# Products of the gated attention's output projection moved between the heads of the last state-space tile, sums of squares one part later, and a projection that waits tile by tile

## The chip, the core and the metric

One core of one Trainium2 chip runs the whole program in one launch. The metric is the device time of one execution in microseconds (us). A core has five engines with queues of their own: PE (TensorE, matmuls), ACT (ScalarE), DVE (VectorE), POOL (GpSimd) and SP (SyncE, which issues DMAs); semaphores order them. TensorE's clock is granted by a throttle, at 2.4 GHz (shown as 1.00) or 1.2 GHz (0.50).

## What is computed

One decoder layer on 592 tokens (16 meta, 512 of a prompt, 8 sequences of 8 sample tokens), in float32. Two mixers run side by side and their outputs are projected together:

```python
o_gla = rmsnorm(o, gla_norm_w) * silu(g)                 # gated linear attention, 512 wide
y = rmsnorm(y_ssd * silu(z), ssd_norm_w)                 # state-space mixer, 512 wide
mix = concatenate([o_gla, y])
h = h + mix @ w_out                                      # 1024 x 1024
h = h + peer(rmsnorm(h, norm2_w), ...)                   # 16384 experts, 16 picks for each of 8 heads
```

The last line is the long part of the program (from about 480 us on); the change lies ahead of it, where `mix @ w_out` is made.

## The kernel before

Tokens lie along the columns: `h`, `xn` and `mix` are 128 x 8 x 592, worked on in two halves of 296 columns. For the mixers the tokens are cut into five tiles, four of 128 and the last, the sample tile, of 80 (16 prompt tokens and the 8 sequences).

The output projection is split over its input. `mix[:, 0:4]` is the attention's half and is ready first; `project_gla(k)` makes part k (of 8 parts of 128 output features) from it: 2 halves x 4 blocks, eight full products of 128x128 by 128x296, into banks 6 and 7. The profile shows each product as two passes, so one part is x16. ScalarE copies part k out of the banks (`copy_gla_out(k)`, semaphore `half_copied`), and part k + 1 may only start then, since it writes the same banks. GpSimd adds the copied parts to the residual `h`, which is loaded again into its place once the state-space output is copied (`y_copied`, then `x_reloaded`). `mix[:, 4:8]` is the state-space half. It is ready after the last tile and a norm: VectorE multiplies by silu(z), ScalarE squares, PE sums the squares with a matmul by ones (`norm_sum`, bank 4 and 5), ScalarE takes the square roots, VectorE the reciprocals and then the normalised values (`norm(1)`, semaphore `normed`). Then `project_ssd(k)` makes part k from it, eight full products again, and VectorE adds them to `h`.

The order on each engine is written out by hand. On PE, before: for tile i the decay matrices of the next tile, `project_gla(i)`, then the eight heads of tile i, two matmuls each. The sample tile's heads are longer: one matmul by `L` (80 columns), one by `H` (16 columns) and eight by `Hsm` (8 columns each, the states of the eight sequences), all with 64 output rows. After the loop:

```python
project_gla(TILES)                       # part 5
pe.wait_ge(y_copied, TILES)
for k in range(4):
    norm_sum(1, k)
project_gla(TILES + 1)                   # part 6
project_gla(TILES + 2)                   # part 7
pe.wait_ge(half_copied, KT)
pe.wait_ge(normed, norm_base[1] + 4)
```

and then `project_ssd(0)` to `project_ssd(7)`, with the state updates of the eight sequences (`to_state`) and the sums of squares of the next norm between them. ScalarE's order is: copies of parts 0 to 5, the four squares and two square roots of `norm(1)`, copies of parts 6 and 7.

Lines of the kernel before: L807 product of `project_gla`, L834 and L836 or L841 the heads, L855 product of `project_ssd`, L795 `to_state`, L565 `norm_sum`, L579 the input projections between the attention's chunks, L1163 `copy_gla_out`, L1059 squares, L1062 square roots, L1354 reciprocals, L1364 normalised values, L1606 the multiplication by silu(z), L1864 GpSimd's additions, L1025 the product of the experts' second stage.

## Time and profile before

| | us |
|---|---|
| median of 3 runs | 2017.6 |
| lowest and highest | 2016.31 and 2018.34 |
| the profiled execution | 2015.8 |
| its span, first to last instruction | 2014.0 |
| PE busy in it | 1979.7 |
| VectorE, ScalarE, GpSimd busy | 1211.4, 636.2, 1105.9 |

The span is the profiled execution's own; what is counted against it is counted against 2015.8. PE is busy nearly all the time, so an engine's busy share tells little here; the views that tell more are the chain of waits (what released each piece of work), the timeline (start, duration, engine, line, and in brackets the idle time before it and what ended it) and the windows (busy time of each engine and the granted clock of PE in a stretch). Where a timeline row has x16, it merges sixteen instructions; its end is modelled for matmuls, so the start of the next row is the better end.

### The profile page before, as it was taken

The page shows a single profiled execution, that of the slowest core. Times are in us where ns is not written, and L with a number is a line of the kernel's source. Part 1 is how long each engine was busy: PE and PEld are TensorE (multiplying, and loading weights), DVE is VectorE, ACT ScalarE, POOL GpSimd, SP SyncE. Part 2 cuts the span into 40 slices and gives each one's busy share as a digit, 9 for nine tenths or more (in the row PEclk, how much of TensorE's full clock was granted, in tenths as well). Part 3 has the DMA queues.
Part 4 walks back from the last instruction along what each step waited for, and adds up shares of the span by engine and source line. Part 5 has one row for each costly group of instructions (what it writes and reads, how often), then busy time and mean ns, then how long its engine had stood idle before and what let it go on. Part 6 is the DMA issues. An engine that isn't in the chain of part 4 may idle for free.

```text
span 2014.0 us, 28921 instructions
## 1 busy us (share of the span) xinstructions
PE 1979.7 (98%) x11021; PEld 1772.3 (88%) x11021; DVE 1211.4 (60%) x2243; ACT 636.2 (32%) x935; POOL 1105.9 (55%) x694
## 2 busy tenths in 40 slices
PE   8999999999999999999999999999999999999997
PEld 4678778868999999999999999998999999999996
DVE  4425365646897787778343441114677777777775
ACT  3324123323333232332323333223333333333332
POOL 0113220222358786888888888865566666666310
PEclk8999999999999999999999999999999999999999
DMA  3396003032335455555555555778999999999971
GB/s 152 107 339 203 32 32 89 1 111 101 102 122 122 131 113 141 120 131 131 130 130 120 127 123 125 173 191 284 320 330 325 328 326 327 324 329 323 332 257 49
DMA packets 237285, 365.17 MB, mean 181 GB/s; under 512 B 87777, under 2 KB 178418, under 8 KB 236530
## 3 DMA queue, kind: packets, MB, share of 16 engines
q1 hardware_dynamic: 163570, 294.37, 43.9%
q0 software_dynamic: 72448, 67.41, 16.2%
q10 hardware_dynamic: 1152, 1.84, 0.3%
q8 instruction: 74, 1.21, 0.2%
q14 instruction: 41, 0.34, 0.0%
HBM read 290.15 MB, written 73.38 MB: 181 GB/s over the span
## 4 chain that ended last, share of the span: by engine, by line
PE 95%; DVE 2%; ACT 1%; DMA 1%; SPq 0%; issue 0%; ACTq 0%; POOL 0%; DVEq 0%; POOLq 0%
PE bank L1025 31%; PE bank L941 30%; PE bank L579 9%; PE bank L950 9%; PE bank L885 2%; PE bank L599 2%; PE bank L855 2%; PE bank L807 1%; PE bank L701 1%; PE bank L565 1%; PE bank L672 1%; PE bank L717 1%; PE bank L932 1%; PE bank L985 1%; PE bank L841 1%; DMA ring<-in_v 1%
## 5 line engine op out<-in xcount | busy, mean ns | idle before, releaser
L1886 POOL DMA_INDIRECT gates_scratch<-gate_val,gate_at x384 | 642.7, 1674 | 139.3 <-issue 115.5
L1025 PE MATMUL bank<-W,vsp 128*128 128x448 f32 x3072 | 624.6, 366 | 2.8 <-DVE W L1767 2.8
L1025 PEld LDWEIGHTS bank<-W,vsp 128*128 128x128 f32 x3072 | 578.1, 188 | 48.8 <-issue 3.0
L941 PE MATMUL bank<-xh,usp 128*128 128x448 f32 x2048 | 593.9, 366 | 0.0
L941 PEld LDWEIGHTS bank<-xh,usp 128*128 128x128 f32 x2048 | 384.7, 188 | 30.7 <-ACT gl L1239 0.4
L941 PE MATMUL bank<-xl,usp 128*128 128x448 f32 x1024 | 374.0, 365 | 0.0
L1652 DVE TENSOR_TENSOR usp<-ring,usp 128x1024 fp32r<-128x1024 f32 x120 | 144.5, 1221 | 329.2 <-ACT usp L1217 329.0
L1762 DVE TENSOR_TENSOR vsp<-ring,vsp 128x1024 fp32r<-128x1024 f32 x128 | 157.0, 1227 | 178.6 <-ACT vsp L1304 178.6
L1905 POOL DMA_INDIRECT picked<-in_v,row_index x128 | 149.5, 1168 | 185.5 <-DVE acc L1781 163.0
L1912 POOL DMA_INDIRECT hid_b<-own_hidden_scratch,hid_index x128 | 189.6, 1481 | 63.7 <-issue 38.7
L941 PEld LDWEIGHTS bank<-xl,usp 128*128 128x128 f32 x1024 | 192.5, 188 | 14.2
L579 PE MATMUL bank<-xn,ring 128*128 128x296 f32 x640 | 202.5, 439 | 0.0
L1239 ACT ACTIVATE gl<-bank 128x448 f32<-128x448 f32 x128 | 69.8, 545 | 398.2 <-PE bank L941 398.1
L950 PE MATMUL bank<-usp,xh 128*128 128x256 f32 x1024 | 194.6, 283 | 0.0
L1304 ACT ACTIVATE vsp<-ring 128x1024 fp32r<-128x1024 f32 x128 | 135.7, 1060 | 185.8 <-PE bank L1025 171.1
L950 PEld LDWEIGHTS bank<-usp,xh 128*128 128x128 f32 x1024 | 163.0, 190 | 0.8
L1781 DVE SCALAR_TENSOR_TENSOR acc<-picked,w_b,acc 128x1024 f32<-128x1024 f32 x126 | 160.6, 1280 | 0.2
L1308 ACT ACTIVATE W<-sq 128x448 fp32r<-128x448 f32 x128 | 74.2, 580 | 233.9 <-DVE sq L1757 230.4
L950 PE MATMUL bank<-usp,xl 128*128 128x256 f32 x512 | 144.8, 283 | 0.0
L1217 ACT ACTIVATE usp<-ring 128x1024 fp32r<-128x1024 f32 x128 | 128.2, 1051 | 0.3 <-DMA ring<-in_u 0.3
L579 PEld LDWEIGHTS bank<-xn,ring 128*128 128x128 f32 x640 | 107.8, 191 | 23.2 <-issue 7.3
L1833 POOL TENSOR_TENSOR E<-E,qT 128x2048 f32<-128x2048 f32 (+1 forms) x7 | 29.1, 4159 | 158.0 <-ACT qT L1068 91.2
(278 smaller groups left out, 2054.3 us busy)
## 6 DMA issues: line engine op xcount, KB each, us to landing
ring<-in_u SPq DMA_DIRECT2D x128, 512.0 KB, 3.7
ring<-in_v SPq DMA_DIRECT2D x128, 512.0 KB, 5.6
hidden_scratch<-gl SPq DMA_DIRECT2D x128, 224.0 KB, 1.9
xn<-hidden_scratch SPq DMA_DIRECT2D x128, 224.0 KB, 5.8
G<-gates_scratch SPq DMA_DIRECT2D x120, 224.0 KB, 4.8
gates_scratch<-zero SPq DMA_DIRECT2D x32, 768.0 KB, 8.7
ring<-in_wproj SPq DMA_DIRECT2D x36, 512.0 KB, 4.3
own_hidden_scratch<-glo SPq DMA_DIRECT2D x64, 128.0 KB, 1.7
```

The source lines that it names most:

```text
L579: mm = pe.matmul(bank[2 * (n % 2) + x][:, 0:half], ring[:, n % 4, k * P:(k + 1) * P], src[:, k, at + x * half:at + (x + 1) * half], start= ...
L941: mm = pe.matmul(bank[b][:, 0:TA], w, src[:, k, 0:TA], start=(k == 0 and w is hi and src is xh), stop=(k == KT - 1 and w is lo))
L950: mm = pe.matmul(bank[b][:, 0:2 * P].rearrange("t (a e) -> t a e", a=2), src[:, k, TA:TP], u, start=(k == 0 and u is hi and src is xh), st ...
L1025: mm = pe.matmul(bank[(k + 4) % 8][:, 0:TA], w, W[:, n % 4, z, :], start=(n == 0 and w is hi and z == 0), stop=(n == NE - 1 and w is lo))
L1217: act.activation(usp[:, u_slot(j), 0, :], ring[:, j, :], ACT.Copy).then_inc(uhi_ready, 1)
L1304: act.activation(vsp[:, n % 4, 0, :], ring[:, n % 4, :], ACT.Copy).then_inc(vhi_ready, 1)
L1652: dve.tensor_tensor(usp[:, u_slot(n), 1, :], ring[:, n % 4, :], usp[:, u_slot(n), 0, :].bitcast(F32), ALU.subtract).then_inc(ulo_ready, 1)
L1762: dve.tensor_tensor(vsp[:, n % 4, 1, :], ring[:, n % 4, :], vsp[:, n % 4, 0, :].bitcast(F32), ALU.subtract).then_inc(vlo_ready, 1)
L1781: ins = dve.scalar_tensor_tensor(acc[:, x % 2, :], picked[:, x % NROW, :], w_b[:, x:x + 1], acc[:, x % 2, :], ALU.mult, ALU.add)
L1886: pool.indirect_dma_start(gates_flat, bass.IndirectOffsetOnAxis(ap=gate_at[0:r, i, x:x + 1], axis=0), gate_val[0:r, i, hh, x - hh * TOPK:x ...
L1905: pool.indirect_dma_start(picked[:, x % NROW, :], None, rows_of_v, bass.IndirectOffsetOnAxis(ap=row_index[:, x:x + 1], axis=0)).then_inc(r ...
L1912: pool.indirect_dma_start(hid_b[:, x:x + 1], None, own_flat, bass.IndirectOffsetOnAxis(ap=hid_index[:, x:x + 1], axis=0)).then_inc(picked_ ...
```

## The change

Three edits, in two of the engine programs. (1) `project_gla` can make a part in pieces, and part 5 is made in six pieces between the sample tile's heads: one product after each of heads 1 to 4, two after each of heads 5 and 6. (2) Behind the tile PE makes part 6 and then the sums of squares, where part 5 stood ahead of them; ScalarE copies part 6 between the squares and the square roots of `norm(1)`. (3) `project_ssd(0)` no longer waits for all four normalised tiles, but before each of its first four products for the tile that this product reads.

```diff
-            def project_gla(k):
+            def project_gla(k, first=0, count=2 * GH):
 
-                pe.wait_ge(ring_loaded[k // 2], 16 * (N_FEAT // 4 + 1))
-                if k >= 1:
-                    pe.wait_ge(half_copied, k)
-                for x in range(2):
-                    for c in range(GH):
-                        a = k % 2 * (D // 2) + c * P
-                        mm = pe.matmul(bank[6 + x][:, 0:HALF], ring[:, k // 2, a:a + P], mix[:, c, x * HALF:(x + 1) * HALF],
-                                       start=(c == 0), stop=(c == GH - 1))
-                mm.then_inc(part_done, 1)
+                if first == 0:
+                    pe.wait_ge(ring_loaded[k // 2], 16 * (N_FEAT // 4 + 1))
+                    if k >= 1:
+                        pe.wait_ge(half_copied, k)
+                for m in range(first, first + count):
+                    x, c = m // GH, m % GH
+                    a = k % 2 * (D // 2) + c * P
+                    mm = pe.matmul(bank[6 + x][:, 0:HALF], ring[:, k // 2, a:a + P], mix[:, c, x * HALF:(x + 1) * HALF],
+                                   start=(c == 0), stop=(c == GH - 1))
+                if first + count == 2 * GH:
+                    mm.then_inc(part_done, 1)
...
+                        if 1 <= hh < SH - 1:
+                            project_gla(TILES, first=hh - 1 if hh < 5 else 2 * hh - 6, count=1 if hh < 5 else 2)
...
                 for x in range(2):
                     for c in range(4):
+                        if k == 0 and x == 0:
+                            pe.wait_ge(normed, norm_base[1] + c + 1)
                         a = k % 2 * (D // 2) + c * P
...
-            project_gla(TILES)
+            project_gla(TILES + 1)
             pe.wait_ge(y_copied, TILES)
             for k in range(4):
                 norm_sum(1, k)
-            project_gla(TILES + 1)
             project_gla(TILES + 2)
             pe.wait_ge(half_copied, KT)
-            pe.wait_ge(normed, norm_base[1] + 4)
...
                     act.activation(sq[:, k % 2, :], src[:, off + k, :], ACT.Square).then_inc(sq_ready, 1)
+                if m == 1:
+                    copy_gla_out(TILES + 1)
                 act.wait_ge(sq_used, norm_base[m] + n)
...
             norm(1, lambda k: act.wait_ge(yz_ready, k + 1))
-            copy_gla_out(TILES + 1)
             copy_gla_out(TILES + 2)
```

The lines behind the edits move by two to six: L807 becomes L808, L834 and L841 become L836 and L843, L855 becomes L861, and on ScalarE L1059, L1062 and L1163 become L1063, L1068 and L1169.

On PE, the first three heads of the sample tile, in the kernel before (each row is a line, the operation, its output and inputs, their shape, and the semaphores that it waits for):

```order
L834 MATMUL bank<-L,Xd 64x80 [waits y_copied,h_updated,xw_ready,hsm_keys_loaded,ct_ready,m_ready]
L841 MATMUL bank<-Ct,H 64x16
L841 MATMUL bank<-Ct,Hsm 64x8 x8
L834 MATMUL bank<-L,Xd 64x80
L841 MATMUL bank<-Ct,H 64x16
L841 MATMUL bank<-Ct,Hsm 64x8 x8
L834 MATMUL bank<-L,Xd 64x80
L841 MATMUL bank<-Ct,H 64x16
L841 MATMUL bank<-Ct,Hsm 64x8 x8
```

and in the changed kernel:

```order
L836 MATMUL bank<-L,Xd 64x80 [waits y_copied,h_updated,xw_ready,hsm_keys_loaded,ct_ready,m_ready]
L843 MATMUL bank<-Ct,H 64x16
L843 MATMUL bank<-Ct,Hsm 64x8 x8
L836 MATMUL bank<-L,Xd 64x80
L843 MATMUL bank<-Ct,H 64x16
L843 MATMUL bank<-Ct,Hsm 64x8 x8
L808 MATMUL bank<-mix,ring 128x296 [waits half_copied,ring_loaded2]
L836 MATMUL bank<-L,Xd 64x80
L843 MATMUL bank<-Ct,H 64x16
L843 MATMUL bank<-Ct,Hsm 64x8 x8
L808 MATMUL bank<-mix,ring 128x296
```

Heads 0 and 1 still stand together; from then on a product of `project_gla(5)` stands behind each head, and the first of them carries the waits that stood at the part's start.

On PE, from the last head to the first product of the state-space projection, before:

```order
L841 MATMUL bank<-Ct,Hsm 64x8 x8
L807 MATMUL bank<-mix,ring 128x296 [waits half_copied,ring_loaded2]
L807 MATMUL bank<-mix,ring 128x296 x7
L565 MATMUL bank<-sq,ones_sb 128x296 [waits sq_ready,y_copied]
L565 MATMUL bank<-sq,ones_sb 128x296
...
L565 MATMUL bank<-sq,ones_sb 128x296 [waits sq_ready]
L565 MATMUL bank<-sq,ones_sb 128x296
L807 MATMUL bank<-mix,ring 128x296 [waits half_copied,ring_loaded3]
L807 MATMUL bank<-mix,ring 128x296 x7
L807 MATMUL bank<-mix,ring 128x296 [waits half_copied,ring_loaded3]
L807 MATMUL bank<-mix,ring 128x296 x7
L855 MATMUL bank<-mix,ring 128x296 [waits ring_loaded0,proj_act,normed,half_copied]
L855 MATMUL bank<-mix,ring 128x296 x7
```

and in the changed kernel:

```order
L843 MATMUL bank<-Ct,Hsm 64x8 x8
L808 MATMUL bank<-mix,ring 128x296 [waits half_copied,ring_loaded3]
L808 MATMUL bank<-mix,ring 128x296 x7
L565 MATMUL bank<-sq,ones_sb 128x296 [waits sq_ready,y_copied]
L565 MATMUL bank<-sq,ones_sb 128x296
...
L565 MATMUL bank<-sq,ones_sb 128x296 [waits sq_ready]
L565 MATMUL bank<-sq,ones_sb 128x296
L808 MATMUL bank<-mix,ring 128x296 [waits half_copied,ring_loaded3]
L808 MATMUL bank<-mix,ring 128x296 x7
L861 MATMUL bank<-mix,ring 128x296 [waits proj_act,normed,ring_loaded0,half_copied]
L861 MATMUL bank<-mix,ring 128x296 [waits normed] x3
L861 MATMUL bank<-mix,ring 128x296 x4
```

Part 6 (the one with ring_loaded3) now comes ahead of the sums of squares, and the single wait for all tiles at L855 has become four waits.

On ScalarE, from the squares of `norm(1)` to the copy of part 7, before:

```order
L1059 ACTIVATE sq<-mix 128x592 [waits yz_ready] x2
L1059 ACTIVATE sq<-mix 128x592 [waits sq_used,yz_ready] x2
L1062 ACT_TABLE_LOAD
L1062 ACTIVATE sq<-bank,eps_sb 128x296 [waits sq_used]
L1062 ACTIVATE sq<-bank,eps_sb 128x296
L1163 ACTIVATE sg<-bank 128x296 [waits part_done]
L1163 ACTIVATE sg<-bank 128x296
L1163 ACTIVATE sg<-bank 128x296 [waits part_done]
L1163 ACTIVATE sg<-bank 128x296
```

and in the changed kernel:

```order
L1063 ACTIVATE sq<-mix 128x592 [waits yz_ready] x2
L1063 ACTIVATE sq<-mix 128x592 [waits sq_used,yz_ready] x2
L1169 ACTIVATE sg<-bank 128x296 [waits part_done]
L1169 ACTIVATE sg<-bank 128x296
L1068 ACT_TABLE_LOAD
L1068 ACTIVATE sq<-bank,eps_sb 128x296 [waits sq_used]
L1068 ACTIVATE sq<-bank,eps_sb 128x296
L1169 ACTIVATE sg<-bank 128x296 [waits part_done]
L1169 ACTIVATE sg<-bank 128x296
```

The copy of part 6 stands ahead of the table load and the square roots.

## Rows read from the trace of the kernel before

**Rows 1.** The page's first part, busy time by engine.
```profile
PE 1979.7 (98%) x11021; PEld 1772.3 (88%) x11021; DVE 1211.4 (60%) x2243; ACT 636.2 (32%) x935; POOL 1105.9 (55%) x694
```

**Rows 2.** The chain of waits, 390 to 480 us: start us, us, what.
```profile
402.59 6.47 PE bank L807 x16
409.08 0.73 ACT E L1163 x2
...
410.53 4.34 PE bank L565 x16
...
419.77 4.24 PE bank L807 x16
...
424.89 4.22 PE bank L855 x16
```

**Rows 3.** Windows, from:to, length, PE busy (count), granted clock, DMA share, GB/s.
```profile
311.00:325.00 14.00, 14.00 (x107) 1.00 0.00 0
...
393.00:394.00 1.00, 1.00 (x19) 0.74 0.00 0
398.00:400.00 2.00, 2.00 (x24) 0.50 0.00 0
...
407.00:408.00 1.00, 1.00 (x5) 0.93 1.05 329
...
1366.00:1370.00 4.00, 1.15 (x9) 0.96 0.97 308
1370.00:1373.00 3.00, 3.00 (x9) 0.50 0.67 248
1373.00:1374.00 1.00, 1.00 (x6) 0.94 0.04 13
```

**Rows 4.** Timeline, the heads of the sample tile and part 5 behind them.
```profile
390.31 0.35 PE L834 MATMUL bank<-L,Xd 80*64 80x80 f32 x2
...
391.48 0.24 PE L841 MATMUL bank<-Ct,H 128*64 128x16 f32 x2
...
393.45 0.30 PE L841 MATMUL bank<-Ct,H 128*64 128x16 f32 x2
...
400.55 0.34 PE L841 MATMUL bank<-Ct,H 128*64 128x16 f32 x2
...
404.65 0.34 PEld L807 LDWEIGHTS bank<-mix,ring 128*128 128x128 f32 x1 [0.16 <-issue]
```

**Rows 5.** Timeline of PE, one chunk of the attention's sample tile.
```profile
312.54 1.26 PE L579 MATMUL bank<-xn,ring 128*128 128x296 f32 x4
...
314.67 0.52 PE L579 MATMUL bank<-xn,ring 128*128 128x296 f32 x1
```

**Rows 6.** Timeline of all engines, from the sample tile to the state-space projection.
```profile
403.58 2.83 DVE L1606 TENSOR_TENSOR mix<-mix,sz 128x592 f32<-128x592 f32 x4
...
413.58 1.28 ACT L1062 ACT_TABLE_LOAD   x1
...
414.71 4.15 PE L807 MATMUL bank<-mix,ring 128*128 128x296 f32 x16
...
415.52 4.04 DVE L1354 RECIPROCAL sq<-sq 128x296 f32<-128x296 f32 x2 [8.32 <-ACT sq L1062]
...
428.95 1.89 PE L795 MATMUL bank<-XWm,btok 80*128 80x256 f32 x8
```

**Rows 7.** Timeline in narrow windows, 412 to 425: additions (POOL) and normalisations (DVE).
```profile
412.32 8.41 POOL L1864 TENSOR_TENSOR h<-h,E 128x592 f32<-128x592 f32 x6 [29.03 <-DMA h<-in_xT]
...
419.60 1.77 DVE L1364 SCALAR_TENSOR_TENSOR mix<-mix,prm,sq 128x592 f32<-128x592 f32 x1
...
420.68 1.98 POOL L1864 TENSOR_TENSOR h<-h,sg 128x592 f32<-128x592 f32 x1
...
421.30 2.00 DVE L1364 SCALAR_TENSOR_TENSOR mix<-mix,prm,sq 128x592 f32<-128x592 f32 x1
...
423.97 0.82 DVE L1364 SCALAR_TENSOR_TENSOR mix<-mix,prm,sq 128x592 f32<-128x592 f32 x1
```

## The prediction

> **What bounds the kernel now.** I read the page first: TensorE is busy for 1979.7 of 2014.0 us [rows 1], so only idle or slow time of TensorE can be won. The chain of waits shows where it lies around the change: from the end of the sample tile at 402.5 us to the first state-space product at 424.9 it runs mostly over PE, with three holes where PE waited for ScalarE: from 409.1 to 410.5, and 0.9 us each before 419.77 and before 424.89 [rows 2]. Then I read the granted clock in windows: it falls in the window of 393 and is back at about 407.1 [rows 3]. PE was busy throughout, and what it had done before the fall was heads of the sample tile alone, ten small matmuls each. Two heads take 1.97 us at 2.4 GHz (391.48 to 393.45), 0.98 each; four take 7.10 at 1.2 GHz (to 400.55), 1.78 each. A full product of 128x296 takes 0.51 us at 2.4 GHz (eight between 424.89 and 428.95) [rows 2, 6]. At 1.2 GHz it takes 0.99: two passes of 0.34 + 0.16 us by its weight loads [rows 4]. Five slow heads lose 0.8 us each and the projection behind them 2.4 (6.47 against 4.06): 6.4 us lie there.
>
> **Edit 1, the eight products of part 5 between the heads.** No instruction is added; eight products move from behind the tile into it, one after each of heads 1 to 4, two after heads 5 and 6. Part 5's first product waits for the copy of part 4, which ScalarE makes while heads 0 and 1 run (0.73 us against 1.97): it costs nothing. ScalarE's copy of part 5 now lies beside head 7 (0.73 and a little for the signal, against 0.98): nothing either, with under 0.2 us to spare. If the clock holds, the tile ends at 390.3 + 8 x 0.98 + 8 x 0.51 = 402.2 with part 5 done, against 409.1 before [rows 2, 4]: 6.9 us ahead.
>
> Does it hold? Before shows both ends. Heads alone, with PE never idle: it fell. The chunks of the gated attention, where two full products (four passes of L579) return every 2.13 us with small matmuls between: 1.00 over 14 us [rows 3, 5]. The new pattern has one product in 1.49 us (0.34 of the time, where the attention has 0.48 and heads alone nothing), from head 5 on two in 2.0 (0.51), but two heads with none at the start. I take full speed, since most of the pattern is nearer to the attention than to heads alone.
>
> **Edit 2, sums of squares one part later.** They now stand behind part 6: 402.2 + 4.1 = 406.3. The first hole goes, since the squares need VectorE's four multiplications, of 0.75 us each from 1.1 us behind the tile on, and these run under part 6. The sums take 4.2 us as before (410.53 to 414.71) and end at 410.5; part 7 follows at once, to 414.6. PE has done by then what it had done by 423.9: 9.3 us ahead [rows 2, 6].
>
> But the next step, the normalised state-space half, hangs on three other engines. Before, the table load for the square roots began 3.05 us after the sums did and lay under the last ones. Now the copy of part 6 stands ahead of it: 406.3 + 3.05 + 0.73 = 410.1, and 1.28 for the load make 411.4, 0.9 behind the sums. The reciprocals begin 0.66 after the load's end and normalisation 4.1 later: 416.1, against 419.6 [rows 6, 7]. The Trainium skill (ScalarE: Activation LUTs, What ACT_TABLE_LOAD costs) puts a change of tables at 2.66 us, a drain included. The trace does not show that drain, since the reciprocals stood 0.66 us behind the load; with it the gain would be 1.4 us smaller.
>
> GpSimd decides the rest. It adds eight parts to the reloaded input from 412.3 on, six in 8.41 us, 1.40 each. Their start hangs on the reload, issued when the tile's output is copied, and stays at 412.1. One normalisation alone takes 0.82 us; the two that met additions took 1.77 and 2.00, and the addition between them 1.98 [rows 7]. The two engines take turns, one pair in about 1.93 us (from the end of the sixth addition, 420.73, to that of the seventh, 422.66). Two of the four met additions before; now only three are done at 416.3 and all four take turns with the rest: they end at 417.0, 418.9, 420.9 and 422.8. Against 424.8 that is 2.0 us, where the start had been 3.5 ahead.
>
> **Edit 3, the projection waits per tile.** Its first four products follow one normalisation each; the fourth and the last four come behind 422.8. At full speed that is 5 x 0.51: 425.4, against 428.95 before, a gain of 3.5 us.
>
> At full speed. But from 414.6 to 422.8 PE has three products, 1.5 us of work in 8.2, with gaps of 2.4, 1.4, 1.5 and 1.4. The nearest rows: a hole of 2.85 us (PE busy 1.15 of 4.00) behind which the clock was at 0.50 [rows 3], and single holes of 1.5 and 0.9 between dense projections, behind which eight products took 4.2 us, as at 2.4 GHz [rows 2]. Three lone products in such a stretch are nearer to the 2.85. So I take a fall near 420. In the rows the clock came back 3.3 us (1369.8 to 1373.1) and 4.6 us (402.5 to 407.1) after dense products had begun. Five products at 0.99 end at 427.8, with the clock back after 3.3 us at 427.0; I take 427.35, a gain of 1.6 us. Behind it PE goes on with the same work, almost without a hole, so the gain is carried to the end. **Sum:** the profiled execution took 2015.8 us (span 2014.0); less 1.6 that is 2014.2. The median of the runs is 1.8 above it: 2017.6 - 1.6 = 2016.0. If the clock never fell the gain is 3.5; if everything ran slow to the end of that projection, 1.1.
>
> **Rivals.**
> A. *The clock holds in the paced projection too.* For it: no single gap is as long as 2.85 us. Against it: four of 1.4 or more in a row. The gain is 3.5 us: 2014.1. The Trainium skill (TensorE: Matmul & The Clock Gate, the table under Why this matters for your kernels) ties a fall to one idle gap between bursts of matmuls; by it this case would come. The fall at 393.5 had no gap before it, which speaks against that reading.
> B. *Slower: the clock still falls between the heads*, where it fell before, in head 2. Then seven products stand in slow time too: 5.3 heads at 1.78 and 7 products at 0.99 from 393.5 on end at 409.9, 7.7 behind 402.2; part 6 loses up to 2.3 more. The reload is issued later too, so nothing is made up: 7.7 + 2.3 - 1.6 = 8.4 us slower, 2026.0. It is decided at the two heads that still stand together; if the clock fell only near head 5, about half. For it: the first 2.5 us behind 390.3 hold one product. Against it: the attention [rows 3, 5].
> C. *GpSimd and VectorE do not take turns.* Then four normalisations take 3.0 us, end at 419.1, PE has no long gap, and the projection ends at 421.7: 7.2 us, 2010.4. For it: the two reciprocals beside additions took 4.04 us and six additions 8.41, evenly. Against it: both slow rows of L1364 and the slow one of L1864 [rows 6, 7].
>
> **How the numbers follow.** About 0.2% (4 us) is what a measurement here can tell from no change; the runs lie 2.0 apart. Forecast 0.57, A 0.21, B 0.16, C 0.06. The forecast gives 1.1 to 3.5 less: nearly all within 0.2%, with 0.06 beyond it for terms that may be off by 1 to 2 us together. A lies on the edge: half faster, half same. C is faster, B slower; 0.01 of the forecast is slower. Faster 0.22, same 0.61, slower 0.17. The range leaves out C and most of B: low 2012.2 is A less 1.9 for the spread and its terms, high 2021.5 is B at half its size.
>
> **What would show it.** In the profile of the changed kernel: granted clock 1.00 from 390 to 414; the last head ending near 402; sums of squares from 406.3 to 410.5; the table load behind a copy, at 410.1; the normalisation four times at 1.7 to 2.0 us beside the additions; PE idle for 6 to 7 us between 414.6 and 422.8; the clock at 0.50 from about 420 to 427; the second state-space product near 429.1, against 430.7. A clock of 0.50 in the heads makes me wrong towards B, normalisations of 0.82 towards C, a full clock behind 420 towards A.

## The result: 0.6% slower, and the profile after

The changed kernel takes 2029.7 us (median of 7 runs, 2027.3 to 2042.1), the kernel before 2016.3 on the same chip (7 runs, 2013.7 to 2025.6); the ratio is 1.0059, 95% interval 1.0035 to 1.0083. The prediction said 2016.0, with a range from 2012.2 to 2021.5, and gave "slower" 0.17. The profiled execution took 2027.3 us (span 2025.5), 11.5 more than that of before. One thing has to be known to read the numbers below: the runs of every kernel here, before and changed, fall into two groups some 12 us apart, in a stage the change does not touch (last section), so medians are compared within the lower group, and the account is made in the traces.

The page's first part, busy time by engine, of the changed kernel, beside [rows 1]:

```profile
PE 1989.8 (98%) x11021; PEld 1776.5 (88%) x11021; DVE 1213.8 (60%) x2243; ACT 636.1 (31%) x935; POOL 1108.4 (55%) x694
```

The same 11021 matmuls are busy for 10.1 us longer. That is not a wait: it is the same matmuls, for the most part at a lower clock, and in an order in which each takes longer (see why the prediction was wrong). Windows of the changed kernel, in the columns of [rows 3] with all engines (PE, PEld, DVE, ACT, POOL busy, granted clock, DMA share, GB/s):

```profile
386.00:392.00 6.00, 6.00 (x58) 4.65 (x57) 1.09 (x3) 0.73 (x2) 0.00 (x0) 1.00 0.00 0
393.00:416.00 23.00, 23.00 (x125) 17.55 (x125) 2.47 (x7) 1.47 (x4) 0.00 (x0) 0.50 0.02 3
416.00:417.00 1.00, 1.00 (x5) 0.81 (x4) 1.00 (x2) 0.64 (x1) 0.00 (x0) 0.89 0.96 358
417.00:429.00 12.00, 10.11 (x41) 7.11 (x39) 5.66 (x6) 4.92 (x9) 4.90 (x4) 1.00 0.89 308
429.00:430.00 1.00, 0.00 (x0) 0.00 (x0) 1.00 (x1) 0.00 (x0) 1.00 (x2) 0.93 0.94 356
430.00:440.00 10.00, 7.86 (x14) 4.21 (x15) 6.12 (x4) 0.00 (x0) 7.41 (x4) 0.50 0.02 8
```

The clock falls in the heads, 3.6 us behind the first of them (before: 3.2), but stays at 0.50 for some 24 us instead of 13.6. It falls a second time at 429.9 us, for 10 us. PE was busy for the whole of the first stretch; when the second began it had been idle since 427.1. The chain of waits of the changed kernel (start us, us, what), beside [rows 2, 4]:

```profile
391.11 0.69 PE bank L808 x2
...
393.62 1.29 PE bank L808 x2
394.90 0.46 PE bank L836 x2
395.36 1.83 PE bank L843 x18
...
404.34 2.27 PE bank L808 x4
...
413.46 5.56 PE bank L808 x16
...
428.41 7.71 DVE mix L1370 x4
436.17 4.69 PE bank L861 x10
```

A lone product between two heads costs 0.69 us at full clock and 1.29 at half, and a pair 2.27. The head behind it takes 2.29 (0.46 and 1.83), where a head of before takes 1.78 at the same clock (start us, us, what):

```profile
395.12 0.21 PE bank L834 x2
395.33 1.57 PE bank L841 x15
```

The tile's first head starts at 388.77 and its last ends at 413.39, with part 5 done: 24.6 us. Before, tile and part 5 took 18.7 (390.31 to 409.05). Then the timelines of the changed kernel, by engine, beside [rows 6, 7]:

```profile
421.71 0.70 ACT L1169 ACTIVATE sg<-bank 128x296 f32<-128x296 f32 x2
422.44 1.28 ACT L1068 ACT_TABLE_LOAD   x1
...
424.34 4.04 DVE L1360 RECIPROCAL sq<-sq 128x296 f32<-128x296 f32 x2 [6.27 <-ACT sq L1068]
428.41 7.70 DVE L1370 SCALAR_TENSOR_TENSOR mix<-mix,prm,sq 128x592 f32<-128x592 f32 x4
...
424.10 9.46 POOL L1870 TENSOR_TENSOR h<-h,E 128x592 f32<-128x592 f32 x6 [42.35 <-DMA h<-in_xT]
...
430.50 1.32 PE L861 MATMUL bank<-mix,ring 128*128 128x296 f32 x2 [3.39 <-DVE mix L1370]
432.33 1.35 PE L861 MATMUL bank<-mix,ring 128*128 128x296 f32 x2 [0.51 <-DVE mix L1370]
...
436.17 4.69 PE L861 MATMUL bank<-mix,ring 128*128 128x296 f32 x10 [0.57 <-DVE mix L1370]
440.70 1.89 PE L795 MATMUL bank<-XWm,btok 80*128 80x256 f32 x8
```

The first state-space product ends at 440.70, where L795 begins: 51.9 us behind the first head of the tile, against 38.6 before (390.31 to 428.95). The 13.3 us are four terms. Tile with part 5: +5.9. Part 6, begun at half clock, 5.47 instead of 4.15: +1.3. Waits of PE between: +0.1. The state-space product, from its first matmul to its end, 10.20 instead of 4.06: +6.1. The sums took 0.1 less. The third and fourth terms are what became of edits 2 and 3. The waits of PE between 409 and 445 us, before and then changed (total, times, longest):

```profile
PE bank L565 <- ACT sq L1059: 1.5, 1, 1.5
PE bank L807 <- ACT sg L1163: 0.9, 1, 0.9
PE bank L855 <- ACT sg L1163: 0.9, 1, 0.9
```

```profile
PE bank L861 <- DVE mix L1370: 5.0, 4, 3.4
```

Three waits for ScalarE, 3.3 us, became one of 3.4 for VectorE, which is the third term, and three short ones that lie in the fourth. Behind that point nothing differs: the experts' second stage starts 940.8 us after this product's end before and 940.6 in the change (1369.8 and 1381.3 us).

### The profile page after: what moved, and what is told of

It reads as the page before. It is cut to its first block, busy times and chain, and to the rows that moved or that the text cites. A ratio compares the mean times of both kernels' runs of the same rounds, so it can differ in the third digit from the quotient of the medians.

```text
span 2025.5 us, 28921 instructions
## 1 busy us (share of the span) xinstructions
PE 1989.8 (98%) x11021; PEld 1776.5 (88%) x11021; DVE 1213.8 (60%) x2243; ACT 636.1 (31%) x935; POOL 1108.4 (55%) x694
## 4 chain that ended last, share of the span: by engine, by line
PE 94%; DVE 3%; ACT 1%; DMA 1%; SPq 0%; issue 0%; ACTq 0%; POOL 0%; DVEq 0%; POOLq 0%
PE bank L1029 31%; PE bank L945 30%; PE bank L579 9%; PE bank L954 9%; PE bank L889 2%; PE bank L599 2%; PE bank L861 2%; PE bank L808 1%; PE bank L701 1%; PE bank L565 1%; PE bank L672 1%; PE bank L717 1%; PE bank L936 1%; PE bank L843 1%; DVE sq L1360 1%; PE bank L989 1%
```

## The experiments

Each kernel was timed beside the kernel before. The table is worked out from the traces: "to product" is the time from the sample tile's first head to the end of the first state-space product (in some traces that head starts at 388.7 to 389.2 us, in others at 390.2 to 390.6, with the same code ahead of it, so I count from it; e3 alone has other code there); "second" is the start of the second stage, "rest" the time from there to the span's end. The last column is the median of a kernel's lower group less that of before in the same session.

| kernel | to product | second | rest | lower group, us against before |
|---|---|---|---|---|
| before | 38.6 | 1369.8 | 644 | 0 |
| changed | 51.9 | 1381.3 | 644 | +12.8 |
| e1 heads only | 49.8 | 1379.4 | 645 | +11.8 |
| e2 rest only | 39.7 | 1370.6 | 656 | +1.4 |
| e3 two per head | 61.3 | 1391.2 | 658 | +23 |
| e4 one each | 54.3 | 1385.6 | 644 | +13.2 |
| e5 filled waits | 56.2 | 1387.5 | 656 | +16 (one run) |
| e6 adds after | 48.5 | 1380.7 | 645 | +10 (groups not clearly apart) |
| e7 four per head | 54.7 | 1386.9 | 644 | +15 |
| e8 before, adds after | 38.6 | 1368.2 | 656 | +0.4 |
| e9 order and bank | 34.8 | 1366.5 | 644 | -4.0 |
| e10 two spares | 51.7 | 1382.4 | 644 | +11.9 |
| e11 fours | 42.0 | 1373.6 | 644 | +1.8 |
| e12 eight mid | 41.7 | 1373.4 | 656 | +3.5 |
| e13 fours and all | 35.3 | 1364.7 | 644 | -5.0 |

In every trace the second stage starts 940.2 to 941.8 us behind the end of the first state-space product, so what happens up to there is what the kernel gets.

**e1, edit 1 alone** (from the change, edits 2 and 3 undone):

```diff
-                        if k == 0 and x == 0:
-                            pe.wait_ge(normed, norm_base[1] + c + 1)
...
-            project_gla(TILES + 1)
             pe.wait_ge(y_copied, TILES)
             for k in range(4):
                 norm_sum(1, k)
+            project_gla(TILES + 1)
             project_gla(TILES + 2)
             pe.wait_ge(half_copied, KT)
+            pe.wait_ge(normed, norm_base[1] + 4)
...
-                if m == 1:
-                    copy_gla_out(TILES + 1)
...
             norm(1, lambda k: act.wait_ge(yz_ready, k + 1))
+            copy_gla_out(TILES + 1)
             copy_gla_out(TILES + 2)
```

> Edit 1 alone: part 5 between the heads, everything behind the tile as before. Theory P (the loss of the change has two shares: slow clock in the heads, and behind the tile a chain over ScalarE, VectorE and GpSimd that edits 2 and 3 lengthened and left uncovered by matmuls): the clock falls at about 392 and stays at 0.50 until some us of dense products behind the tile; the tile ends 10 to 12 us later than in the kernel before with part 5 done; normalisations start about 17 us behind the tile's end, two of them slow; the first state-space product ends 3 to 6 us later than before, so the time is 3 to 6 us over before. Rival Q (all of the loss is edit 1): 11 to 13 us over before. Rival R (edit 1 costs nothing by itself, edits 2 and 3 do it): within 1 us of before, clock 1.00 through the heads.

Ratio 1.0048 (1.0019 to 1.0077). The clock is at 0.50 from before 393 until after 419 us. PE in this kernel's timeline:

```profile
416.08 6.02 PE L565 MATMUL bank<-sq,ones_sb 128*128 128x296 f32 x16 [2.64 <-ACT sq L1062]
...
434.47 4.22 PE L859 MATMUL bank<-mix,ring 128*128 128x296 f32 x16 [3.25 <-issue]
```

Eleven of the 13 us come with edit 1 alone, which is the size of Rival Q; Theory P had 3 to 6. The sums, which have lost part 5 as their cover, wait 2.6 us and then run at half clock for their first 3.4 us; the state-space product stands together and runs at full clock, though it too follows a wait of 3.25 us.

**e2, edits 2 and 3 alone**, part 5 behind the tile as before:

```diff
-                        if 1 <= hh < SH - 1:
-                            project_gla(TILES, first=hh - 1 if hh < 5 else 2 * hh - 6, count=1 if hh < 5 else 2)
...
+            project_gla(TILES)
             project_gla(TILES + 1)
```

> Edits 2 and 3 without edit 1: the eight products of part 5 stand behind the tile again, then part 6, the sums of squares, part 7, and the projection that waits per tile. Theory P: the heads are as before (clock falls near 393.5, tile ends near 402.5), the sums begin near 414 instead of 410.5, since part 6 is now ahead of them, roots 0.9 behind the sums; normalisations start near 424 and are mostly past the additions (0.82 each), the first state-space product ends near 429.6 against 428.95: 0 to 2 us over before. Rival Q: 0. Rival R: 8 or more over before.

Ratio 1.0014 (0.9985 to 1.0043).

```profile
423.72 6.35 PE L859 MATMUL bank<-mix,ring 128*128 128x296 f32 x16 [3.11 <-DVE mix L1369]
429.90 1.89 PE L795 MATMUL bank<-XWm,btok 80*128 80x256 f32 x8
```

No gain, and a loss of the size that Theory P had (0 to 2 us): from the tile's end to the product's end it takes 28.4 us, before 26.4. Waits of 0.9 and 3.1 stand in place of 1.5, 0.9 and 0.9, and the product, at half clock for 3.4 us from 425.3 on, takes 6.2 instead of 4.1.

**e3 and e4, how many products stand between the heads.** e3 has two behind every head (parts 4 and 5), e4 one behind every head, the first two included:

```diff
-                if i > 0:
+                if 0 < i < TILES - 1:
...
+                        project_gla(TILES - 1 + hh // 4, first=2 * (hh % 4), count=2)
```

```diff
-                        if 1 <= hh < SH - 1:
-                            project_gla(TILES, first=hh - 1 if hh < 5 else 2 * hh - 6, count=1 if hh < 5 else 2)
+                        project_gla(TILES, first=hh, count=1)
```

> The changed kernel, but part 4 is spread too: two products behind each of the eight heads, parts 4 and 5, none in a block ahead of the tile. Theory P with density (the clock wants more matmul work than one product a head): clock 1.00 through the heads, sample tile with both parts done about 5 us sooner than before had them; but PE then waits for the normalisations as in the changed kernel (two slow spells are possible there): 2 us under to 2 us over before. If two products a head are too few as well, all sixteen products run slow: 14 us or more over before.

> The changed kernel, but one product of part 5 behind each of the eight heads, so that no two heads stand together. Rival H (the prediction's case B had it decided by the two bare heads at the start): clock 1.00 through the heads, tile ends near 402, time 0 to 4 us under before. Theory P with density: one product a head is too little wherever it stands, the clock falls near 392 and stays at 0.50 to the end of the tile, 11 to 14 us over before.

Ratios 1.01 (1.0059 to 1.0142) and 1.0063 (1.0035 to 1.0092). A window and two rows of PE's timeline in e3:

```profile
391.00:427.00 36.00, 35.09 (x175) 25.80 (x175) 4.54 (x10) 2.62 (x6) 0.00 (x0) 0.50 0.10 28
```

```profile
403.22 2.34 PE L808 MATMUL bank<-mix,ring 128*128 128x296 f32 x4
405.49 0.53 PE L836 MATMUL bank<-L,Xd 80*64 80x80 f32 x2
```

The clock does not come back among pairs of products; a head with its pair takes 4.56 us, half of it in full products (2.27). Whether pairs would have kept it up is not shown: without part 4 ahead of the tile PE waited 2.29 us for its first head, and the clock fell 1.7 us behind that wait, sooner than in any other trace. In e4 it fell 3.2 us behind the first head, as in before (change: 3.6), so the two bare heads at the start did not decide it.

**e7, four products per head**: e4 with three spare ones, into a bank that nobody reads:

```diff
+                        for j in range(3 if hh > 0 else 0):
+                            pe.matmul(bank[3][:, 0:HALF], ring[:, 2, j * P:(j + 1) * P], mix[:, j, 0:HALF], start=True, stop=True)
                         project_gla(TILES, first=hh, count=1)
```

> One full product of part 5 behind every head as in the run with one each, and ahead of it, from the second head on, three spare products of the same form into a bank that nobody reads: four products between heads. Theory D (what holds the clock is how much of TensorE's time goes to full products, and one or two per head were too few): the clock stays at 1.00 through the tile or comes back inside it, a head with its four products takes 2.3 to 2.6 us, and the tile ends some 19 us after its start. Rival S (between heads nothing holds or restores it): 0.50 from 392 us on, 4.6 us or so per head with its products, the tile ends some 36 us after its start, and the second stage starts 10 us later than with one each (1395 us).

Ratio 1.01 (1.0068 to 1.0131). Windows of e7:

```profile
394.00:397.00 3.00, 3.00 (x7) 2.04 (x7) 0.00 (x0) 0.00 (x0) 0.00 (x0) 0.50 0.03 5
397.00:398.00 1.00, 1.00 (x9) 0.41 (x8) 0.00 (x0) 0.00 (x0) 0.00 (x0) 0.83 0.00 0
398.00:434.00 36.00, 32.84 (x213) 24.72 (x211) 9.50 (x13) 6.81 (x13) 7.86 (x6) 1.00 0.34 118
```

The clock falls near 394 and is back at 397.3, still inside the first group of four (393.72 to 397.60), and then holds to the tile's end. So what stands between the heads does decide whether it comes back; one and two did not bring it back. The 21 spare products themselves, at some 0.5 us, cost more than the clock gives. A head with four takes 3.48 us; I had written 2.3 to 2.6 from a wrong price for a product (0.28). The right price, 0.51, makes 3.02; the other 0.46 come of the alternation itself, 0.3 of it in the head. The tile took 28 us where I had 19.

**e11 and e12, part 5 in blocks**: two groups of four behind heads 2 and 5, or all eight behind head 3 (the first head is head 0), in place of the change's own condition, the rest as in the change:

```diff
+                        if hh in (2, 5):
+                            project_gla(TILES, first=4 * (hh // 5), count=4)
```

```diff
+                        if hh == 3:
+                            project_gla(TILES)
```

> The changed kernel, with part 5 in two groups of four products, behind the third and the sixth head, instead of one or two products behind six heads. Theory B4 (full products must stand together to count; the run with four per head came back to 1.00 after one group): the clock is at 0.50 for at most 5 us inside the tile, which ends 13 to 16 us after its start with part 5 done (change: 24.6 us; before, part 5 behind it: 18.7 us), second stage near 1370 us. Rival M (only the share of full products in the whole stretch counts, which is the change's own): 0.50 from 3 us after the start on, the tile ends 23 to 25 us after its start, second stage near 1381 us.

> The changed kernel, with all eight products of part 5 behind the fourth head. Theory B4: the clock falls some 3 us after the tile's start, the block brings it back within about 4.5 us (before: part 5 from 402.5 us, clock back at 407.1), and the last four heads run at 1.00 nearly to their end: the tile ends 15 to 17 us after its start (before with part 5: 18.7 us), and the second stage starts near 1370 us or sooner. Rival M: 0.50 from 3 us on to the end of the tile, 22 to 24 us.

Ratios 1.001 (0.9982 to 1.0038) and 1.0016 (0.999 to 1.0042). Windows of e11:

```profile
394.00:397.00 3.00, 3.00 (x7) 2.04 (x7) 0.00 (x0) 0.00 (x0) 0.00 (x0) 0.50 0.02 5
397.00:398.00 1.00, 1.00 (x8) 0.41 (x8) 0.00 (x0) 0.00 (x0) 0.00 (x0) 0.82 0.00 0
398.00:400.00 2.00, 2.00 (x44) 2.00 (x42) 0.00 (x0) 0.00 (x0) 0.00 (x0) 1.00 0.00 0
...
401.00:404.00 3.00, 3.00 (x6) 2.07 (x7) 0.00 (x0) 0.00 (x0) 0.00 (x0) 0.50 0.00 0
```

The same eight products and the same eight heads as in the change now take 16.5 us (e12: 15.9) instead of 24.6, and 2.2 less than tile and part 5 took before. In e11 the clock still falls twice, but the low stretches, 3.4 us each, lie almost wholly in the blocks (393.73 to 397.61 and 400.88 to 404.69) and each ends inside its block; in e12 it falls at the fourth head and is back inside the block (at 400.7), and the last four heads run at full clock. Theory B4 had 13 to 16 us for e11, with the clock low for at most 5 where it was 6.8 in all, and 15 to 17 for e12. The share of products in the tile is the change's own, so what counted is that they stand together. Yet in both the product ends more than 3 us later than before, counted from the first head: four slow normalisations (7.7 and 7.8 us) and the second fall give the gain back.

**e5 and e10, the second fall.** In the change, spare products while PE waits for the normalised tiles; 14 and then 4 each in e5, two each time in e10:

```diff
-                wait_proj_evacuated(pe, n)
+                wait_proj_evacuated(pe, n + 1 if k == 0 else n)
...
                         if k == 0 and x == 0:
+                            for j in range(2):
+                                pe.matmul(bank[2 * ((n + 1) % 2)][:, 0:HALF], ring[:, 0, j % 4 * P:(j % 4 + 1) * P],
+                                          mix[:, j % 4, 0:HALF], start=True, stop=True)
                             pe.wait_ge(normed, norm_base[1] + c + 1)
```

> The changed kernel, with spare products into a bank that nobody reads while TensorE waits for the normalised tiles: 14 ahead of the first, 4 ahead of each of the other three (0.28 us each at 2.4 GHz, from a part of eight in 2.25 us). Theory F (the second fall of the clock, at about 430 us, comes of these waits and costs what follows): the clock stays at 1.00 from 420 us on, the last wait still ends at 436.2 us, and the first state-space projection ends near 437.6 us instead of 440.7, the second stage of the experts starts some 3 us sooner (1378 us), and the median is some 3 us under the change. Rival G (the waits do not bring the clock down, the slow end has another cause): the clock falls near 430 us all the same, and the first state-space projection ends at 440 us or later.

> As the run with filled waits, where a spare product turned out to cost 0.52 us and not 0.28, so that they overran; here two spare products ahead of each of the four waits. Theory F (the second fall of the clock comes of these waits): no stretch at 0.50 after the tile, the first state-space projection ends 25.3 us after the last head instead of 27.3 (last normalisation 22.7, then five products of 0.52), second stage 2 us sooner than in the change for the same start of the tile. Rival G: the clock falls in it all the same, and it ends 27 us or more after the last head.

Ratios 1.0113 (1.0075 to 1.015) and 1.005 (1.0022 to 1.0078). In e5 the spares overran. They gave the price of a full product among its like, in its timeline:

```profile
429.74 7.24 PE L860 MATMUL bank<-mix,ring 128*128 128x296 f32 x28 [0.81 <-ACT sg L1172]
```

14 products in 7.24 us, 0.52 each (my 0.28 was wrong, and the trace of before had it as 0.51), and no low clock behind part 6. In e10 the window from the sums on reads

```profile
421.00:445.00 24.00, 21.42 (x83) 14.85 (x82) 14.35 (x11) 6.29 (x11) 12.80 (x8) 1.00 0.39 138
```

Full clock throughout: with the waits filled for the most part, the second fall does not come. The waits brought it, and not the lone products in them: in the change the clock fell at 429.9, 2.8 us behind the end of part 7 with PE idle, and 0.6 ahead of the first lone product; in e3, e4, e7 and e12 it fell in the same wait, after 2.4 to 3.1 us. What follows a fall goes with its length: 6.8 to 10.2 us where lone products come (those four, the change and e11), 3.4 where the eight products stand together (e2 and e6). That a wait of this length always does it is not so: e1's of 3.25 us had no fall behind it. From the end of part 7 the product takes 11.8 us (430.1 to 441.94) against 13.6 in the change (427.1 to 440.70): 1.8 us is what the second fall costs, near the 2 expected. It shows no net gain, since in that trace the first low stretch lasted 3.4 us longer (to 420.6), and part 6 with it: the product ends 26.7 us behind the last head, where Theory F had 25.3 and Rival G 27 or more.

**e6 and e8, the turns of GpSimd and VectorE.** GpSimd's additions wait until the four normalisations are done, in the change (e6) and in the kernel before (e8):

```diff
+            pool.wait_ge(normed, norm_base[1] + 4)
             for k in range(KT):
                 pool.wait_ge(half_copied, k + 1)
```

> The changed kernel, with GpSimd's additions held back until VectorE has made the four normalisations of the state-space half. Theory T (the two engines take turns, which makes a normalisation 1.93 us instead of about 0.83): the four normalisations take 3.3 us instead of 7.7, the last product of the first half starts near 431.7 us instead of 436.2, and the first state-space projection ends between 433.5 us (clock kept) and 436 us (clock down), 5 to 7 us sooner than in the change; second stage near 1375 us, median 5 us or so under the change. Rival N (the long normalisation is VectorE's own time or another partner's): they still take 7 us or more and nothing moves. Rival V (the additions become the bound): the evacuation of the first or second state-space projection waits for GpSimd, and the gain is given back there.

> The kernel before, with GpSimd's additions held back until the four normalisations of the state-space half are done, and nothing else changed. Theory T: the normalisations take 3.3 us instead of 5.2, the wait for the last of them ends 1.9 us sooner (422.9 us), the first state-space projection ends near 427.0 us instead of 428.95, second stage 1.9 us sooner (1367.9 us), median 1 to 3 us under before. Rival V: the additions, then 421 to 434 us instead of 412 to 426, hold up the evacuations (429.2 us and 434.9 us before), and nothing is gained.

Ratios 1.0063 (1.0039 to 1.0088) and 1.0023 (0.9998 to 1.0049). VectorE and PE in e6, then in e8:

```profile
431.69 3.07 DVE L1370 SCALAR_TENSOR_TENSOR mix<-mix,prm,sq 128x592 f32<-128x592 f32 x4
...
432.67 6.37 PE L861 MATMUL bank<-mix,ring 128*128 128x296 f32 x16 [2.29 <-DVE mix L1370]
```

```profile
418.25 3.07 DVE L1364 SCALAR_TENSOR_TENSOR mix<-mix,prm,sq 128x592 f32<-128x592 f32 x4
...
423.46 4.25 PE L855 MATMUL bank<-mix,ring 128*128 128x296 f32 x16 [0.82 <-ACT sg L1163]
```

The four take 3.07 us instead of 7.70 and 5.19: the additions were what stretched them. In the change that gives 3.9 us from the tile's end to the product's end (27.3 to 23.5), less than the 5 to 7 expected, since the clock falls in the product here too. In the kernel before it gives nothing: the product waits for ScalarE's copy of part 7 at the same place as before. The last normalisation and that copy had ended together, and I had written only of the one.

**e9, the waits for ScalarE removed as well** (on e8): squares ahead of the copy of part 5, part 7 into banks 2 and 3, so that it and the state-space product need not wait for a copy:

```diff
-                if k >= 1:
+                if 1 <= k < KT - 1:
                     pe.wait_ge(half_copied, k)
...
-                        mm = pe.matmul(bank[6 + x][:, 0:HALF], ring[:, k // 2, a:a + P], mix[:, c, x * HALF:(x + 1) * HALF],
+                        mm = pe.matmul(bank[(2 if k == KT - 1 else 6) + x][:, 0:HALF], ring[:, k // 2, a:a + P], mix[:, c, x * HALF:(x + 1) * HALF],
...
-            pe.wait_ge(half_copied, KT)
...
                 if k == 0:
+                    pe.wait_ge(half_copied, KT)
                     to_state(4, 0)
...
+                    if m == 1 and k == 1:
+                        copy_gla_out(TILES)
...
-            copy_gla_out(TILES)
             norm(1, lambda k: act.wait_ge(yz_ready, k + 1))
```

> Built on the run with the additions held back in the kernel before: ScalarE makes the first two squares ahead of its copy of part 5, and part 7 goes into banks 2 and 3, so that it does not wait for the copy of part 6, nor the first state-space projection for that of part 7. In that run this projection began 22.6 us after the last head and ended 26.7 us after it (before: 22.4 and 26.4), with TensorE waiting 1.49 us for squares and 0.91 and 0.82 us for the two copies. Theory C (once the additions are out of the way these waits of TensorE for ScalarE are the bound): the projection begins about 20.1 us after the last head and ends 24.2 us after it, the second stage starts some 2.4 us sooner than before if the heads start at the same time (1367.4 us), median 1.5 to 3 us under before. Rival R (roots, reciprocals and normalisations bound it at the same place): a wait of 2 us for VectorE comes in their place and nothing is gained.

2008.4 to 2024.4 us over 12 runs, median 2014.1 against 2017.7; the ratio 0.9985 (0.996 to 1.001) mixes the two groups and does not exclude 1. Within the lower group it is 2012.1 (7 runs) against 2016.15 (24 runs), and the trace has the second stage 3.3 us sooner.

```profile
413.29 8.14 PE L807 MATMUL bank<-mix,ring 128*128 128x296 f32 x32
...
418.17 3.07 DVE L1365 SCALAR_TENSOR_TENSOR mix<-mix,prm,sq 128x592 f32<-128x592 f32 x4
...
421.30 4.25 PE L855 MATMUL bank<-mix,ring 128*128 128x296 f32 x16
425.39 1.89 PE L795 MATMUL bank<-XWm,btok 80*128 80x256 f32 x8
```

Parts 6 and 7 and the product stand without a wait, and the normalisations (to 421.24) end just ahead of it. The product ends 23.0 us behind the last head, where I expected 24.2 and before had 26.4, and 34.8 behind the first, 3.8 sooner than before. Theory C holds, and the gain is larger than expected. It is shown by the trace and by the lower group, not by the ratio of all runs.

**e13, both together**: the groups of four of e11 with the held additions and the banks of e9, and the copy of part 6 behind the roots again. Of e9's order on ScalarE nothing is needed here, since part 5 is done and copied inside the tile.

> Part 5 in two groups of four products as in the run with fours, and with it what made the run with order and bank faster: the additions held back behind the normalisations, part 7 into banks 2 and 3, and no copy of a part ahead of the roots. That run ended its first state-space projection 34.8 us after the first head of the tile began, with TensorE never waiting long. Theory K (the chain behind the sums becomes the bound): tile with part 5 in 16.5 us, part 6 and sums 8.2 us, roots and reciprocals and normalisation start 4.8 us behind the sums, TensorE idle for about 1.5 us after part 7, the projection paced by normalisations of 0.77 us and ending 34.9 to 35.5 us after the first head: no faster than the run with order and bank. Rival W (the 2.3 us that the groups save in the tile come through): it ends 32 to 33 us after the first head, the second stage starts some 2 us sooner than in that run (1364.5 us), and the median is 5 us or more under before.

```profile
418.75 3.07 DVE L1369 SCALAR_TENSOR_TENSOR mix<-mix,prm,sq 128x592 f32<-128x592 f32 x4
...
419.74 4.91 PE L861 MATMUL bank<-mix,ring 128*128 128x296 f32 x16 [1.72 <-DVE mix L1369]
```

Median 2015.0 (2010.7 to 2031.1, 12 runs) against 2016.3, ratio 0.9997 (0.997 to 1.0023); the lower group is 2011.2 against 2016.2. The product ends 35.3 us behind the first head, inside Theory K's 34.9 to 35.5 and no sooner than in e9. The 2.2 us saved in the tile turn up as PE's wait of 1.72 for the first normalised tile and a product of 4.74. Its second stage starts 1.8 us sooner than e9's, but its tile began 1.4 sooner, and another 0.8 comes between the product and that stage, where all traces scatter by as much; that it beats e9 is not shown.

## Why the prediction was wrong

*Edit 1, "Does it hold?" and "I take full speed".* This is the step that failed. The granted clock fell at the heads with one product between them, as it had with none, and stayed at 0.50 for 24 us. I ranked the pattern by its share of full products and put it nearer to the attention, where "two full products" return "every 2.13 us" [rows 5]. e3 has half its time in pairs of full products and never came back inside the tile. The share left out what else stands in a chunk of the attention, in the timeline of before:

```profile
313.63 0.51 PE L717 MATMUL bank<-qz,Ssm 128*128 128x16 f32 x4
314.08 0.66 PE L701 MATMUL bank<-V,khm 80*64 80x128 f32 x8
```

Counted in passes, as the profile does, there are beside the two full products eight of 128 columns, 0.59 us of the 2.13; a head of the sample tile has two of 80 columns, and the rest are of 16 and 8. Whether it is these that hold the clock there was not tested; e7, e11 and e12 show that four or eight products together bring it back. The prediction named the right rival (B) and gave it 0.16.

*Edit 1, the prices in the sum.* The prediction took 0.98 us for a head (1.78 at half clock) and 0.51 (0.99) for a product, prices from rows where each stands among its like. A head that a product follows takes 1.29 us at full clock (e7, 401.07 to 402.36) and 2.29 at half, and a lone product 0.69 and 1.29. In the timelines the first matmul of a head begins before the last ones of the head ahead of it (before: 391.29 and 391.34); beside a product there is no such overlap. So each of the six places costs some 0.5 us at full clock and 0.8 at half. Had the clock held, the 6.9 us of edit 1 would have been about 4, an estimate from these rows.

*Rival B's size and its "decided at the two heads".* It was priced at 8.4 us and came to 13.3. The miss is in the tile with part 5: 24.6 us, where B had 19.6 (390.3 to 409.9). From 393.55 to 413.39 five heads and seven products took 19.8 us, where B's prices make 15.8; the other 1.1 us lie ahead of that, in the first three heads and their product. Behind the tile B had 27.5 us to the product's end and it took 27.3, which is partly luck: part 6 lost 1.3 instead of 2.3, and what follows it took 0.8 more. That two bare heads decide it is refuted by e4.

*Edit 2.* Its steps came as worked out: the hole before the sums went, the sums' end at 422.96 and the table load's at 423.72 lie 0.8 us apart (0.9 predicted), the reciprocals begin 0.6 behind the load, with no drain to be seen, and the normalisation 4.1 later. Its gain went where the prediction said that it would be lost, to GpSimd: the four normalisations took 7.7 us, 1.93 each, where I had let the first pass with 0.9 and took 6.7. e6 and e8 show this cause directly.

*Edit 3.* The second fall of the clock came as predicted, but sooner and for another reason. The prediction had three lone products among gaps of at most 2.4 us bring it about, 5 us behind part 7. The first wait was 3.4 us, since the first normalisation met an addition too, and the clock fell in that wait, before any lone product. It lasted 10 us, not 7: the first four products came 1.9 us apart, and the clock was back some 3.9 us after the dense ones began at 436.17. e2 says that edits 2 and 3 alone cost about 1 us (2 from the tile's end), where the forecast for all three edits had a gain of 1.6. Rivals A and C are out, C by its own measurement. The page that A leaned on, in the Trainium skill (TensorE: Matmul & The Clock Gate, the table under Why this matters for your kernels), ties a fall to an idle gap. The second fall agrees with it, 2.8 us into a gap; the first does not, since it came with PE busy throughout in before, in the change and in all the runs but e3, and neither does e1's gap of 3.25 us without a fall.

*What stays open.* How three full products between heads would do, and whether pairs would keep up a clock that has not yet fallen; neither was tried. The tile's first head starts at 388.7 to 389.2 us in four traces (change, e1, e8, e13) and, e3 apart, at 390.2 to 390.6 in the others. This goes with where the clock was low ahead of it: in those four for 6.8 us from about 37 and again from about 228 us, in the others for 10.2 from about 35 and for 3.4 from about 233. Why one or the other comes is open.

## What to carry to other kernels

Full products that are moved in among small matmuls one at a time did not keep TensorE's clock up here, and neither one nor two at a time brought it back; four together did. Each place where the two kinds meet also costs some 0.5 us at full clock, in the product and in the group of small matmuls ahead of it, so take no price from rows where each stands among its like. Move products in blocks of four or more, or leave them together. Before paying for an earlier start, read every chain that ends at the point where it would be used: here a normalisation that another engine stretched, and a bank's copy that ended in the same tenth of a microsecond. Two waits that end together have to be removed together (e8 gave nothing, e9 gave 3.8 us), and a wait of TensorE of some 3 us can cost a second fall of the clock (here in seven of the eight traces with one of 3 us or more ahead of the product), and lone products behind it go with a longer one.

## What the runs showed of the hardware

VectorE and GpSimd slow each other: four normalisations of 128x592 on VectorE take 3.07 us alone, and 6.6 to 7.8 where all four fall beside GpSimd's additions of the same size; two additions beside them take 3.88 us in the change, where six with no normalisation beside them take 8.40 in e8, 1.40 each. The load of the table for the roots took 1.28 us, and the reciprocals stood 0.6 behind its end, in before and in the change alike.

The second stage of the experts, 3072 matmuls of one form, runs at one of two paces per execution, both at a granted clock of 1.00. A window of before (lower group), then one of e2 (upper group), PE busy and its count, clock, DMA share, GB/s:

```profile
1450.00:1490.00 40.00, 40.00 (x199) 1.00 0.93 324
```

```profile
1450.00:1490.00 40.00, 40.00 (x195) 1.00 0.94 318
```

2% over this stage is the 12 us between the groups (rest of 644 or 656 us in the table). It shows in no clock, wait or queue that I read, and its cause is open.
